# Two-layer diffusion trunk on one core: head norms one step later, out-projection weights split inside the last attention steps

## What is computed

```python
def diff_attention(q, k, v, lam):                  # per block of 128 queries
    s = jnp.einsum('bqhmd,bkhmd->bhmqk', qi, k) * scale
    p = jax.nn.softmax(s, axis=-1)
    w = p[:, :, 0] - lam * p[:, :, 1]
    return jnp.einsum('bhqk,bkhe->bqhe', w, v)
def diff_head_out(o, subln_g, lambda_init):
    return rmsnorm(o, subln_g) * (1.0 - lambda_init)   # per head
def spatial_gating(u, gv, ln_g, ln_b, w_s, b_s):
    vn = layernorm(gv, ln_g, ln_b)
    mixed = jnp.einsum('gpq,bcqge->bcpge', w_s, vc) + b_s
    return u * mixed
...
a_lat = diff_head_out(diff_attention(q_l, k_all, v_all, lam), subln_g[l], lambda_init)
s_lat = spatial_gating(u_l, g_l, sg_ln_g[l], sg_ln_b[l], sg_w[l], sg_b[l])
o_lat = jnp.concatenate([a_lat, s_lat], axis=-1) @ w_out[l]
x_lat = x_lat + ms[2] * rmsnorm(o_lat, post_mix_g[l])
```

## Time and profile before

| | us |
|---|---|
| median of 3 runs | 1877.4 (1876.48 to 1880.33) |
| the profiled execution | 1876.53 |
| its span, first to last instruction | 1874.7 |
| PE, DVE, ACT busy | 1726.1, 1415.7, 1099.6 |
| mean granted TensorE clock | 0.968 of full speed |

### The profile page before, as it was taken

One profiled execution on the slowest core, in us unless ns is written; L12 is line 12 of the kernel. 1 busy time (PEld: TensorE's weight loads), 2 busy tenths in 40 slices (PEclk: granted clock), 3 DMA queues, 4 the chain that ended last, 5 costly groups with the idle time before them and its releaser, 6 DMA issues.

```text
span 1874.7 us, 24261 instructions
## 1 busy us (share of the span) xinstructions
PE 1726.1 (92%) x8008; PEld 1397.5 (75%) x8008; DVE 1415.7 (76%) x1647; ACT 1099.6 (59%) x1409; POOL 71.1 (4%) x91
## 2 busy tenths in 40 slices
PE   6998798999999969874999999999999999999993
PEld 3765586878878858564888888888888888888883
DVE  3846647565754487653899999999999999999994
ACT  3334534222222253543788888888888888888883
POOL 0110300000010000121000000000000000000000
PEclk9999998999999989986999999999999999999997
DMA  9945134655674427243899999999999999999992
GB/s 321 254 129 182 55 127 128 220 197 186 212 228 139 159 64 277 83 146 102 315 383 362 395 374 374 392 352 396 378 369 392 356 391 382 366 394 358 387 379 89
DMA packets 229520, 505.78 MB, mean 270 GB/s; under 512 B 16377, under 2 KB 47249, under 8 KB 229185
## 3 DMA queue, kind: packets, MB, share of 16 engines
q1 hardware_dynamic: 225216, 493.30, 73.5%
q0 software_dynamic: 4224, 11.47, 2.4%
HBM read 497.34 MB, written 19.96 MB: 276 GB/s over the span
## 4 chain that ended last, share of the span: by engine, by line
issue 54%; PE 34%; DVE 7%; ACT 3%; DMA 2%; SPq 0%; POOL 0%; POOLq 0%; ACTq 0%; DVEq 0%
PE ps L600 10%; PE ps L602 10%; PE ps L601 10%; DVE w_lo L1371 1%; DMA raw<-in_ffn_w 1%; PE ps L833 1%; DVE att L1624 1%; PE ps L669 1%; DMA raw<-in_ada_w 1%; DVE xs L1550 1%; ACT w_hi L1072 1%; DVE hT_lo L1523 1%; ACT pr L1189 0%; PE ps L797 0%; PE ps L821 0%
## 5 line engine op out<-in xcount | busy, mean ns | idle before, releaser
L1371 DVE TENSOR_TENSOR w_lo<-raw,w_hi 128x1024 fp32r<-128x1024 f32 x570 | 684.9, 1222 | 208.3 <-ACT w_hi L1072 174.0
L1283 ACT ACTIVATE w_hi<-raw 128x1024 fp32r<-128x1024 f32 x448 | 473.9, 1062 | 105.9 <-PE ps L602 105.9
L600 PE MATMUL ps<-w_hi,he_hi 128*128 128x512 f32 x896 | 354.4, 396 | 0.7 <-DVE he_lo L1773 0.7
L602 PE MATMUL ps<-w_hi,he_lo 128*128 128x512 f32 x896 | 350.1, 391 | 0.0
L601 PE MATMUL ps<-w_lo,he_hi 128*128 128x512 f32 x896 | 349.6, 390 | 0.0
L1371 DVE TENSOR_TENSOR w_lo<-raw_more,w_hi 128x1024 fp32r<-128x1024 f32 x224 | 273.9, 1225 | 45.7 <-ACT w_hi L1283 26.2
L1283 ACT ACTIVATE w_hi<-raw_more 128x1024 fp32r<-128x1024 f32 x224 | 237.7, 1062 | 53.5 <-PE ps L602 53.5
L1072 ACT ACTIVATE w_hi<-raw 128x1024 fp32r<-128x1024 f32 x122 | 128.6, 1063 | 215.1 <-PE ps L602 190.2
L602 PEld LDWEIGHTS ps<-w_hi,he_lo 128*128 128x128 f32 x896 | 168.6, 188 | 36.0
L600 PEld LDWEIGHTS ps<-w_hi,he_hi 128*128 128x128 f32 x896 | 168.7, 188 | 34.9 <-issue 1.0
L601 PEld LDWEIGHTS ps<-w_lo,he_hi 128*128 128x128 f32 x896 | 168.8, 188 | 33.9
(11 more groups left out here) (229 smaller groups left out, 2002.9 us busy)
## 6 DMA issues: line engine op xcount, KB each, us to landing
raw<-in_moe_w SPq DMA_DIRECT2D x448, 512.0 KB, 6.0
raw_more<-in_moe_w SPq DMA_DIRECT2D x224, 512.0 KB, 6.0
raw<-in_ada_w SPq DMA_DIRECT2D x96, 512.0 KB, 4.7
raw<-in_ffn_w SPq DMA_DIRECT2D x66, 512.0 KB, 5.0
raw<-in_w_in SPq DMA_DIRECT2D x40, 512.0 KB, 6.7
raw<-in_w_out SPq DMA_DIRECT2D x16, 512.0 KB, 4.6
yrows<-in_x SPq DMA_DIRECT2D x8, 512.0 KB, 7.6
xe<-xrows SPq DMA_DIRECT2D x8, 512.0 KB, 6.4
```

The costliest lines, as they stand in the source:

```text
L600: pe.matmul(o, lh, rh, start=start, stop=False)
L602: return pe.matmul(o, ll, rh, start=False, stop=stop)
L1283: act.activation(w_hi[:, s % SPL, :], expert_raw(i), ACT.Copy).then_inc(hi_done, 1)
L1371: dve.tensor_tensor(w_lo[:, s_ % SPL, :], src, w_hi[:, s_ % SPL, :].bitcast(F32), ALU.subtract)\
```

## The change

Six things are done, in both layers:

- ACT copies `wT` at the start of the next step, behind `osq` of the item before, instead of ahead of it.
- `head_norm` is cut in two. `head_mean` stays at the end of the block's last step; the square root goes to ACT's next step, ahead of Exp, and the rest to the end of DVE's next step.
- The gate's root and reciprocal move one step ahead (`NORM_AT` 10 to 9 and 6 to 5), away from the head's root, so each has its own change of tables; in layer 0 three of the four `mix` steps and three of the four `gate` steps move ahead.
- The table for the last root is loaded by a Sqrt of a constant in step n (16 and 8), where the Exps are over.
- The first four `w_out` units are split in steps n and n+1, two in each, on ACT ahead of that step's `osq`, on DVE behind its copy and gate.
- `turn_cat` of pieces 4 to 7 goes ahead of unit two (index 1) instead of unit three; the last head root stands between the copies of pieces 3 and 4.

```diff
-NORM_AT = {0: 10, 1: 6}
-MIX_AT = {0: (11, 13, 15, 16), 1: (7, 8)}
-GATE_AT = {0: (12, 14, 16, 17), 1: (8, 9)}
+NORM_AT = {0: 9, 1: 5}
+MIX_AT = {0: (10, 11, 13, 15), 1: (7, 8)}
+GATE_AT = {0: (11, 12, 14, 16), 1: (8, 9)}
...
# PE, project_out
-                    if i % 2 == 0:
-                        turn_cat(l, range(2 * i, 2 * i + 4))
+                    if i < 2:
+                        turn_cat(l, range(4 * i, 4 * i + 4))
...
# ACT, attend
+                def head_root(i):
+                    b = ORDER[l][i]
+                    o = slice(HEADS * b, HEADS * b + HEADS)
+                    act.wait_ge(sg("o ms"), NB * l + i + 1)
+                    act.activation(st2[:, 32:48][:, o], st2[:, 16:32][:, o], ACT.Sqrt).then_inc(sg("o rt"), 1)
...
+                    if t > LAG:
+                        i = t - LAG - 1
+                        nk = 512 if its[i][0] < NLAT else 256
+                        act.wait_ge(sg("wT ps"), 16 * l + i + 1)
+                        if i >= 2:
+                            act.wait_ge(sg("pv"), 16 * l + i - 1)
+                        act.activation(wT[:, i % 2, 0:nk], ps[:, BANK_W, 0:nk], ACT.Copy).then_inc(sg("wT"), 1)
+                    if t > LAG + HEADS and (t - LAG - 1) % HEADS == 0:
+                        head_root((t - LAG - 1) // HEADS - 1)
+                    if t == NORM_AT[l]:
+                        act.wait_ge(sg("ln ms"), l + 1)
+                        act.activation(st[:, 44:44 + nb], st[:, 40:40 + nb], ACT.Sqrt).then_inc(sg("ln rt"), 1)
+                    if t == n:
+                        stage_end[0] = in_end[l + 1]
+                        act.activation(st2[:, 127:128], cst[:, C_ONES:C_ONES + 1], ACT.Sqrt)
...
-                    if LAG <= t < n + LAG:
-                        i = t - LAG
...
-                        act.activation(wT[:, i % 2, 0:nk], ps[:, BANK_W, 0:nk], ACT.Copy).then_inc(sg("wT"), 1)
+                    if t in (n, n + 1):
+                        split_upto(at["out", l, 0][2 * (t - n) + 1].s)
...
                 for j, k in enumerate(CAT):
-                    if j % 2 == 0:
-                        split_upto(at["out", l, 0][0].s + j // 2)
+                    if j == 4:
+                        head_root(nb - 1)
...
# DVE, attend
+                    if t == NORM_AT[l]:
+                        dve.wait_ge(sg("ln rt"), l + 1)
+                        dve.wait_ge(sg("params in"), 16 * (11 + 3 * l))
+                        dve.reciprocal(st[:, 36:36 + nb], st[:, 44:44 + nb]).then_inc(sg("ln rstd"), 1)
...
+                    if t in (n, n + 1):
+                        split_upto(at["out", l, 0][2 * (t - n) + 1].s)
+                    if t > LAG + HEADS and (t - LAG - 1) % HEADS == 0:
+                        head_norm(l, (t - LAG - 1) // HEADS - 1)
                     if t > LAG and (t - LAG - 1) % HEADS == HEADS - 1:
-                        head_norm(l, (t - LAG - 1) // HEADS)
+                        head_mean(l, (t - LAG - 1) // HEADS)
+                split_cat(l, nb, range(4))
+                head_norm(l, nb - 1)
```

More of the change, by code:

```diff
@@ L1665, in split_cat, with head_mean @@
                         .then_inc(sg("catT"), 1)
+            def head_mean(l, n):
+                b = ORDER[l][n]
+                o = slice(HEADS * b, HEADS * b + HEADS)
+                dve.wait_ge(sg("o sq"), 16 * l + HEADS * (n + 1))
+                dve.tensor_scalar(st2[:, 16:32][:, o], st2[:, 0:16][:, o], 1.0 / P, EPS, ALU.mult, ALU.add).then_inc(sg("o ms"), 1)
             def head_norm(l, n):
-                b, nb = ORDER[l][n], len(ORDER[l])
+                b = ORDER[l][n]
                 o = slice(HEADS * b, HEADS * b + HEADS)
                 keep = 1.0 - (0.8 - 0.6 * math.exp(-0.3 * l))
-                ss, ms, rt, rstd = (st2[:, k:k + 16][:, o] for k in (0, 16, 32, 48))
-                dve.wait_ge(sg("o sq"), 16 * l + HEADS * (n + 1))
+                rt, rstd = (st2[:, k:k + 16][:, o] for k in (32, 48))
                 dve.wait_ge(sg("o"), 16 * l + HEADS * (n + 1))
[L1675 to L1679, removed]
                 dve.wait_ge(sg("o rt"), NB * l + n + 1)
```

## The result

The change took the median from 1878.77 us (1876.27 to 1882.34) to 1860.36 us (1856.84 to 1864.41): ratio 0.9907, 95% interval 0.9892 to 0.9922. In a second set of runs it was 0.9912 (0.9892 to 0.9933), 15 us by the medians. The forecast was 1864.9, so 12.5 us were expected and 15 to 18 came; the median lies inside the range of 1859 to 1872, near its lower end. The profiled execution of after took 1856.84 us, the lowest of its runs, with a span of 1855.0 against 1874.7.

A forecast was written before the change was run, and what follows sets the result against it. The prediction took a chain across ACT and DVE, not matmul work, to bound the attention steps and tails. Its terms, -4.6 -1.5 -0.8 -4.0 -0.9 -0.7 = -12.5 us, gave 1864.9 from 1877.4; range 1859 to 1872, the forecast's own 1860 to 1868.5.

The forecast's parts named there:

- Term 1: Layer 0's attention steps up to Exp(15): 4.6 us shorter, ends -3.6 and -5.6.
- Term 2: Layer 0's tail, Exp(15) to first out-projection matmul: 1.5 us shorter, ends -2.4 and -0.1.
- Term 3: Layer 0's out-projection: PE's wait at the second turn goes, 0.8 us shorter.
- the clock: Layer 0's out-projection: granted clock stays at 0.90 behind a half idle tail, gain 0, best end -2.75 us.
- Terms 4 to 6: Layer 1: steps to Exp(7) -4.0 us, tail to first out-projection matmul -0.9, the out-projection's wait at 831.05 -0.7.
- Steps that give little: Rival, chance 0.10: POOL's norm slows the weights and mix(1) waits for gate(0); only -6.4 us in all, 1871.
- a tail that gives nothing: Rival, chance 0.08: early splits cost what they save in both layers' tails; -8.6 us in all, 1869.
- Table changes that bound the block ends: Rival, chance 0.02: each table change 1.38 us longer, at block ends and tails; -3.7 us in all, 1873.7.
- The slower case: Rival, chance 0.05: new short waits drop PE to 1.2 GHz in layer 0's steps 11 to 15; +26 us, 1890.

The follow-up runs named there:

- mix_spread: The change, with layer 0's mix in steps 10, 12, 14, 16 and gate in 11, 13, 15, 17; 1859.31 us, ratio 0.9902.
- after_again: The changed kernel itself, run once more with nothing altered; 1861.91 us, ratio 0.9912 against the kernel before.
- turn_late: The change, with pieces 4 to 7 turned ahead of unit three again; 1861.05 us, ratio 0.9914.
- units_late: The change, with the first four w_out units split between the pieces again, in both layers; 1862.71 us, ratio 0.9924.
- norm_only: The kernel before, with only the change's wT order, cut head_norm and last root's place; 1861.81 us, ratio 0.9912.
- before_warm: The kernel before, with 54 more matmuls on constants on PE in three waits of layer 0's tail; 1873.86 us, ratio 0.9978.

## Why the forecast was right, and where its terms were off

The sign, the range and the order of the terms held: the cut `head_norm` carries the steps, the root's load left the tail, the turn lost its wait. The size held narrowly: 1860.36 is 0.4 above the lower end of the forecast's own 1860 to 1868.5, and most misses lie on one side, which the forecast called unlikely (its ends add up to -21.05, not -20.9). With matmuls on constants in both kernels the rows give 13.9, the medians 7.8 or 12, against the forecast 12.5. Of what came on top, the 2.68 of layer 0's out-projection is the clock; the rest is in part open.

- **Term 1** (-4.6, measured -6.21, beyond its end of -5.6). Exp(11) was put at 186.0 and came at 185.29, in part by luck: weights(10) began at 180.59, not 181.84, as the square of item 7 came at 180.08 and not at before's 181.22; then DVE took 4.70 to Exp(11) beside POOL, not 4.2. The wait for gate(0) was put at 1.4 and was 1.51. The step that failed is the pace of steps 11 to 15. I took PE's times around step 10 from before, where rows at half speed delay it; in after PE runs step 10 at full clock (its half-speed rows lie at 168 to 173, ahead of Exp(9), which still comes 54.46 behind Exp(0), in before 54.81), and mix(1) starts at 186.91 instead of 188.65. Then I let PE pace Exp(13): 199.6, measured 198.69. mix_spread shows that it does not, and Exp(14) to Exp(15) was 6.20 instead of 7.2. How much of the 1.6 is clock and how much that wrong pace, no run separates.
- **Term 2** (-1.5, measured -3.01). The two pieces of the working were right: 11.39 to the last square against 11.9, then 2.35 against 2.4. The 0.9 set aside for a falling clock and late DVE copies was not needed in this profile; in after_again the clock did fall and the tail took 15.31, -1.44. The early splits give little of it, 0.33.
- **Term 3** (-0.8, measured -0.98 by turn_late), **and the clock** of the out-projection (0 taken, best end -2.75, measured -2.68). This is the largest miss. I wrote that the tail stays half idle and so the clock as it was. The tail is half idle still, 7.85 of 13.80 us, but neither profile of the changed kernel has a half-speed row in that stretch, and over all runs with a clock on record its mean is 0.966 in before (36 runs) and 0.969 in the change (12). What keeps it up stays open. PE's single pauses in the tail are shorter, 0.98 to 2.66 instead of up to 3.99, but behind a pause of 2.57 units_late has half-speed rows there and norm_only none. In layer 1 the pause of 1.08 (row at 804.10 above) did not help: seven rows of 0.63 follow it, where five follow before's 4.33.
- **Terms 4 to 6** (-4.0, -0.9, -0.7; measured -3.52, -1.15, -0.70) hold; of term 6 turn_late gives 0.96, and the half-speed rows just named take some back. The gate's earlier norm on POOL cost Exp(6) 1.55 us against Exp(5), more than the 0.9 that I allowed; norm_only, without it, has 30.05 from Exp(3) to Exp(7).
- **The rivals.** Steps that give little and a tail that gives nothing are out by terms 1, 4, 2 and 5 above. Table changes that bound the block ends are out: a load takes 1.28, the root starts 1.29 behind the load's start and Exp(15) 1.65 behind that of the next; with another 1.38 for each change, as this rival had it, Exp(15) could not have come at 209.46. The Trainium skill (ScalarE: Activation LUTs, "What ACT_TABLE_LOAD costs") adds a drain of about 1380 ns to each change of tables; the rows here show none. The slower case did not come: the new wait of 1.51 in step 11 is followed by rows at full speed.
- **Not forecast:** 1.45 us in places that the change leaves alone; two runs of one kernel differ by more there (4.5 in the mixer, after_again against after).

## What to carry to other kernels

Read a stage's granted clock before its waits are priced: where PE pauses, a shorter chain can also give back half-speed rows behind the pause (layer 0 here, not layer 1), and durations taken from such rows must not be carried into the new order. Test that part by itself, with matmuls on constants inside the waits; here they alone were worth about as much as a careful reordering, and the two together 24 to 27 us. Try the parts of a reordering alone, too: here one of them, the cut norm, gave all that the time can tell. When a copy is moved behind an instruction that waits for another engine, look at the last items too, where nothing else covers that wait.

## What the runs showed of the hardware

- Most of the spread between runs of one kernel goes with TensorE's granted clock: before's runs differ by 9.2 us between mean clocks of 0.969 and 0.964, after's first six by 7.6 between 0.972 and 0.967. The same wait can have either end: in layer 0's mixer, 2.75 us in before with rows of 0.47 and 0.40 behind it, and 2.75 in before_warm with 0.76 and 0.63.
- A float32 128x128 matmul on constants took 0.23 us at full clock, and each stands as two rows in the trace's count (52 for the 26 behind the turn).
- DVE beside POOL: four SCALAR_TENSOR_TENSOR on 128x128 took 2.58 us in after at 187.28, with POOL's norm beside them, against 1.14 at 211.06 without.
